# A gathered buffer holds rows of four heads for 32 tokens, TensorE sums all of V in four column tiles, VectorE makes every convolution

## The reference, cut to what matters

```
xbc = silu(causal_depthwise_conv(xbc, conv_w, conv_b))      # 4 taps, 4096 channels
...
h   = layer_norm(ALPHA * h + merged @ w_out)
...
hid = einsum('td,thkd->thk', xb, expert_u[ib])              # t tokens, 8 heads, 16 experts
act = gelu(hid) * gate
out = einsum('thk,thkd->td', act, expert_v[ib])
h   = layer_norm(ALPHA * h + out)
```

## Time and profile before

| what | value |
|---|---|
| median of 3 runs | 3692.26 us (3683.3 to 3696.73) |
| span of the profiled execution | 3689.4 us |
| PE busy | 3041.9 us, 82% |
| DVE busy | 2784.4 us, 75% |
| ACT, POOL busy | 1041.1 us, 2079.6 us |
| DMA moved | 1394.61 MB, 378 GB/s over the span |

### The profile page before, as it was taken

How to read it: one execution, slowest core, us unless ns; L and a number is a source line. 1 busy time by engine, 2 the same in 40 slices (tenths; PEclk the granted TensorE clock), 3 DMA queues, 4 the chain that set the end, 5 groups by cost and what they waited for, 6 DMA issues and landing times.

```text
span 3689.4 us, 41001 instructions
## 1 busy us (share of the span) xinstructions
PE 3041.9 (82%) x13528; PEld 2256.1 (61%) x13528; DVE 2784.4 (75%) x5841; ACT 1041.1 (28%) x2599; POOL 2079.6 (56%) x1839
## 2 busy tenths in 40 slices
PE   8984988988889899999988889999978974664665
PEld 7884877777778557877776537887765521221221
DVE  3318974988885898888777888888777886667666
ACT  5511542234331223444312114444211111111101
POOL 0004543566554667776666677677666676555553
PEclk9997998989999999999999999999999997887778
DMA  6658999999898999999999999999999999999997
GB/s 244 212 228 320 398 407 363 382 360 359 325 340 341 411 391 411 402 411 397 381 411 412 403 393 412 410 393 403 393 388 409 372 408 401 421 421 421 421 421 326
DMA packets 316546, 1394.61 MB, mean 378 GB/s; under 512 B 35376, under 2 KB 40880, under 8 KB 251824
## 3 DMA queue, kind: packets, MB, share of 16 engines
q0 software_dynamic: 262656, 1073.86, 73.4%
q1 hardware_dynamic: 52384, 313.42, 21.6%
q10 hardware_dynamic: 1296, 4.72, 0.3%
HBM read 1387.66 MB, written 4.19 MB: 377 GB/s over the span
## 4 chain that ended last, share of the span: by engine, by line
PE 30%; DMA 23%; POOL 9%; DVE 9%; issue 6%; ACT 2%; DVEq 1%; ACTq 0%; POOLq 0%
PE main L637 13%; DMA rowbuf<-ev,idx 9%; POOL rowbuf L594 6%; PE vbank L723 5%; DMA rowbuf<-euv,idx 4%; PE main L645 3%; DVE acc L1667 3%; DMA ring<-euv,idx 3%; PE main L848 2%; DVE rowbuf L1641 2%; PE main L833 2%; PE turn L708 2%; DMA xT<-euv,idx 2%; DMA merged<-euv,idx 2%; DMA rowbuf<-eu,idx 1%
## 5 line engine op out<-in xcount | busy, mean ns | idle before, releaser
L594 POOL DMA_INDIRECT rowbuf<-eu,idx x714 | 845.2, 1184 | 895.0 <-DVE hdot L1641 347.7
L594 POOL DMA_INDIRECT rowbuf<-ev,idx x713 | 773.7, 1085 | 323.1 <-issue 193.9
L1641 DVE CUSTOM_DVE_ANT_0 rowbuf<-rowbuf,hb 128x1024 f32<-128x1024 f32 x620 | 758.1, 1223 | 139.9 <-DMA rowbuf<-eu,idx 73.5
L637 PE MATMUL main<-xT,ring 128*128 128x256 f32 (+1 forms) x4480 | 802.8, 340 | 49.4 <-ACT mm L1104 38.9
L637 PEld LDWEIGHTS main<-xT,ring 128*128 128x128 f32 x4480 | 722.1, 193 | 124.1 <-issue 54.4
L723 PE MATMUL vbank<-rowbuf,vdiag 128*128 128x512 f32 x1152 | 602.4, 660 | 174.2 <-DMA rowbuf<-ev,idx 90.5
L1667 DVE SCALAR_TENSOR_TENSOR acc<-rowbuf,hact,acc 128x1024 f32<-128x1024 f32 x509 | 655.0, 1287 | 98.9 <-DMA rowbuf<-ev,idx 89.8
L723 PEld LDWEIGHTS vbank<-rowbuf,vdiag 128*128 128x128 f32 x1152 | 225.8, 210 | 490.6 <-issue 326.0
L1053 ACT ACTIVATE vdiag<-ident,hact 128x128 f32<-128x128 f32 x441 | 165.3, 396 | 515.2 <-DVE hact L1650 339.2
L833 PE MATMUL main<-late,ring 128*128 128x256 f32 (+1 forms) x1280 | 239.5, 352 | 36.0 <-issue 27.2
L833 PEld LDWEIGHTS main<-late,ring 128*128 128x128 f32 x1280 | 214.4, 203 | 60.4 <-issue 30.8
(11 more groups left out here) (249 smaller groups left out, 4136.3 us busy)
## 6 DMA issues: line engine op xcount, KB each, us to landing
ring<-wblocks SPq DMA_DIRECT2D x280, 1024.0 KB, 8.1
rowbuf<-eu,idx POOLq DMA_INDIRECT x714, 11.8
rowbuf<-ev,idx POOLq DMA_INDIRECT x713, 11.6
pw<-poolw SPq DMA_DIRECT2D x20, 256.0 KB
h_out<-acc ACTq DMA_DIRECT2D x8, 512.0 KB, 7.5
xT<-xt SPq DMA_DIRECT2D x3, 1024.0 KB, 16.8
zy<-x SPq DMA_DIRECT2D x3, 1024.0 KB, 13.9
craw_ln<-ln1g SPq DMA_DIRECT2D x5, 512.0 KB, 14.2
```

Of the source, the lines that this page charges most:

```text
L594: pool.indirect_dma_start(rows[r], None, (eu, ev)[table], bass.IndirectOffsetOnAxis(ap=idx[c % 2][:, u, k:k + 1], axis=0)).then_inc(row_re ...
L637: last = pe.matmul(dst_[:, ct * tc:(ct + 1) * tc], w[:, k, ct * P:(ct + 1) * P], src[:, k, 0:tc], start=(k == 0), stop=(k == KD - 1))
L1641: last = dve.tensor_tensor_reduce(r, r, h, 1.0, 0.0, ALU.mult, ALU.add, hdot[:, g % 2, k:k + 1])
```

## The change

**Layout.** A gathered buffer no longer holds one row for each of 128 tokens but rows of four heads for 32 tokens: partition 32a + m holds head a's row of token 32j + m. Four buffers j = 0 to 3 together (a quad, `QUAD`) cover the 128 tokens. The number of gathers, their bytes and their order in U and V stay.

**V.** VectorE makes from the weights of 16 slots one tile `spots` (128 x 512: for each slot 32 columns with the weight on the token's place). `sum_quad` on TensorE multiplies each of the four buffers by its 32 columns and adds into partitions 32j to 32j + 31 of `vbank`: eight matmuls of 128 x 512 moving data with 32 columns of weights each, for four buffers. At the start of a tile TensorE adds h itself into `vbank`. VectorE's `sum_row` and the diagonals of ScalarE are gone; `finish_tile` copies the banks.

**U.** `dot` now needs h in the new layout: `hp`, four parts j of 128 x 1024. TensorE makes each part with eight matmuls into `hbank` (`copy_rows`), ScalarE copies the two banks out (`copy_out`). Part j of the next tile is made when the dots that read the old one are done; `places_of_copies` puts it at the first place where the scan does not use `hbank`. The last tile has its own copy in `late`, so the paired rows have 14 buffers instead of 16.

**Experts and gates.** `choose` leaves expert numbers and gates by token in `choice`; TensorE moves them to the new layout (`move`, 16 small matmuls for each tile and half) and VectorE copies them out (`collect`). For the second half this comes in part A of the next chunk.

**Convolutions.** `convolve` and `conv_weights` are gone: chunks 3 and 4 do as chunks 0 to 2.

**Steps.** `WIDTHS` of chunk 3 goes from (124, 26, 16, 40, 38) to (128, 28, 16, 42, 42), so `END` goes from 780 to 792.

```diff
-WIDTHS = ((128, 28, 16, 42, 24), (40, 6, 6, 12, 12), (88, 16, 10, 34, 32), (124, 26, 16, 40, 38), (128, 28, 16, 42, 42))
+WIDTHS = ((128, 28, 16, 42, 24), (40, 6, 6, 12, 12), (88, 16, 10, 34, 32), (128, 28, 16, 42, 42), (128, 28, 16, 42, 42))
...
+            def copy_rows(t, j, scanned, moves):
+
+                if 0 < t < TILES - 1:
+                    pe.wait_ge(row_free, t * TILE - TOPK + QUAD * (j + 1))
+                pe.wait_ge(h_ready, t + 1)
+                pe.wait_ge(y_free, scanned + 1)
+                pe.wait_ge(st_used, scanned + STATE)
...
+                for half in range(2):
+                    n = 2 * (t * QUAD + j) + half
+                    if n >= 2:
+                        pe.wait_ge(hp_ready, n - 1)
+                    for a in range(QUAD):
+                        last = pe.matmul((ybank, stbank)[half][a * 32:(a + 1) * 32, :], ident[:, j * 32:(j + 1) * 32],
+                                         hb[:, t % NT, half * 512:(half + 1) * 512], start=True, stop=True)
+                    last.then_inc(hp_made, 1)
...
-            def convolve(c, j, n):
-
-                pe.wait_ge(conv_raw, (c - FILL) * 4 * AJ + j * 4 + n + 1)
...
-                first = q == PE_ORDER[0] or PE_ORDER[n - 1] // TILE < t
-                if first and t:
-                    pe.wait_ge(vsum_read, t)
-                pe.wait_ge(vdiag_ready, n + 1)
-                pe.wait_ge(ready, landed)
+            def sum_quad(q):
+
+                t, g = q // TILE, q // TOPK
...
+                pe.wait_ge(spots_ready, groups_before(q) + 1)
+                for j in range(QUAD):
+                    _, ready, landed = row(1, q + j)
+                    pe.wait_ge(ready, landed)
                 for half in range(2):
-                    last = pe.matmul(vbank[half][:, :], vdiag[:, n % DIAGS, :], r[:, half * 512:(half + 1) * 512],
-                                     start=first, stop=False, skip_group_check=True)
+                    for j in range(QUAD):
+                        r, _, _ = row(1, q + j)
+                        last = pe.matmul(vbank[half][j * 32:(j + 1) * 32, :], spots[:, g % 2, q % TOPK + j, :],
+                                         r[:, half * 512:(half + 1) * 512], start=False, stop=False, skip_group_check=True)
                 last.then_inc(row_free_pe, 1)
...
-                for t in range(nt):
-                    to = ds(t * PH + i * 4, 4)
-                    last = dve.tensor_copy(idx[c % 2][:, to, :], self_[:, t:n_u:nt, :])
...
+            def collect(c, i):
+
+                dve.wait_ge(moved, c * 2 + i + 1)
```

More of the change, by code:

```diff
@@ L140, in where, with order_rows @@
     return c, tile - FIRST[c], q // TOPK - FIRST[c] * PH
[L143 to L173 removed]
+def order_rows():
+    order, at = [], 0
@@ L174, in assign_rows @@
     for p in range(PAIRED + 1):
-        steps = [(0, p)] if p < PAIRED else []
+        if p < PAIRED:
+            order.append((0, p, False, p + 1))
         while at < PAIRED and step_of_v(at) == p:
-            steps.append((1, at))
+            order.append((1, at, True, at // QUAD + 1))
             at += 1
-        for table, q in steps:
-            by_pe = table == 1 and on_pe[q]
-            count[by_pe] += 1
-            order.append((table, q, by_pe, count[by_pe]))
-    pairs = []
@@ L220, in step_of, with freed @@
     return step_of_v(q) if table else q
+def freed(n):
+    table, q, _, _ = ORDER[n]
+    return step_of_quad(q) if table else q
 def guest_span(c, g):
@@ L596, in _ @@
                                         ).then_inc(row_ready[r], 16)
-            for n, (q, _, _) in enumerate(BOTH):
-                (c, _, u), k = where(q), q % TOPK
+            for n, q in enumerate(range(PAIRED, PAIRS)):
+                (c, _, u), k = where(q), column(0, q)
                 r = n % BOTHS
@@ L948, in _ @@
                 front_d(c)
+            move(NC - 1, 1, (NC, 0, 0))
+            for j in range(QUAD):
+                copy_rows(TILES - 1, j, scans(NC, 0, 0), NC * 2)
             until(PAIRS + LEAD2)
@@ L1067, in until @@
                 for o in range(at, p):
-                    for n, (_, first, begin, _) in enumerate(BANKED):
-                        if not first and o == begin - SETTLE + 1:
-                            bank_h(n)
                     g, k = divmod(o - 18, TOPK)
@@ L1282, in front_d @@
                 score(0, 3)
+                until(o(16))
+                if c == 0:
+                    for j in range(QUAD):
+                        copy_out(0, j)
                 until(o(35))
@@ L1318, in _ @@
                 front_d(c)
+            until(END)
+            for j in range(QUAD):
+                copy_out(TILES - 1, j)
             until(PAIRS + LEAD2 + 16)
```

468 lines of the change are left out of this document (208 added, 260 removed).

## The result

The changed kernel takes 3827.55 us (median of 4 runs, 3824.51 to 3837.86) against 3688.31 us (median of 4, 3683.3 to 3696.73) before: a ratio of 1.0384, 95% interval 1.0363 to 1.0405. The prediction of 3673 us was wrong, in sign too, and the time lies just above its range. The profiled execution has a span of 3827.1 us.

A forecast was written before the change was run, and what follows sets the result against it. It took the front to bound 694 to 1207 us and memory the paired rows, with engines and DMA close from 1406 to 3111. Terms summed to -19 us, giving 3673 us; 8-in-10 range 3640 to 3825.

The forecast's parts named there:

- start and later indices: Kernel start, `move` and `collect` ahead of the first gather: +4 us; first half of chunk 2's indices: +1.
- chunk 1: 390 to 630 us: 12 nearly all new quads, 24 us, on a TensorE idle for 37 of 240 us: +3.
- chunk 2, part A: New quads and copies of h against fewer waits and a quicker clock: 388 us for 390, -2.
- chunk 2, C and W: 6.5 quads, 13 us, replace 4 buffers' 8 us on a TensorE without idle time: +2.
- 1406 to 3111 us: Chunks 3 and 4, memory-bound: 682 MB at 406 instead of 400 GB/s, 1680 us for 1705, -25.
- paired rows: Paired rows, bound by memory at 421 GB/s: 14 buffers instead of 16 still leave several in flight, 0.
- tail: After the last dot: four sums of 5.3 us become `spots`, a quad and a copy, -2 us.
- What bounds the kernel: Whole kernel: front bounds 694 to 1207 us, engines and DMA close from 1406 to 3111, memory bounds paired rows at 421 GB/s.
- The quad: TensorE's sums of V: four buffers, 16 passes, taken as 2.0 us, between 1.7 side by side and 6.9 one by one.
- I take 406: Chunks 3 and 4, 1406 to 3111 us: engine relief lifts the rate from 400 to 406 GB/s, -25 us.
- rival (3): Single rows: V buffers held 8 to 10 us longer, fewer in flight, 392 GB/s, +35 instead of -25, 3733 us; chance 0.08.
- Its sign: From chunk 3 on: a rate below 397 GB/s with POOL waiting for TensorE would show held buffers.

The follow-up runs named there:

- `FILL` 5: Kernel before with VectorE also making the convolutions of chunks 3 and 4, nothing else changed: 3770.31 us, ratio 0.9979.
- The kernel with both costs: Kernel before, V buffers reused only after all four of a quad are read, dots always reading h from SBUF: 3896.75 us, ratio 1.0325; earlier run 3899.65.

## Why the prediction was wrong

Its terms beside what the two traces show (differences of the table's first two columns, taken before rounding; the other parts add 2 us ahead of chunk 1 and 4 us in chunk 2's D):

| term | forecast | measured |
|---|---|---|
| start and later indices | +5 | -1 |
| chunk 1 | +3 | +10 |
| chunk 2, part A | -2 | +20 |
| chunk 2, C and W | +2 | +19 |
| 1406 to 3111 us | -25 | +87 |
| paired rows | 0 | +1 |
| tail | -2 | -4 |

**What bounds the kernel**: right as far as it went, that from chunk 3 on it is memory, and that more TensorE time there is worth little. **The quad** of 2.0 us: right (1.92). So was TensorE's load in parts A (383 forecast, 395 and 388 measured) and that VectorE would fall to about 265 (272). `move` and `collect` are hidden: POOL's wait for the first indices is 279.6 us, as in the earlier trace rows. That 14 paired buffers do as well as 16: right.

**The step that failed** is "I take 406". It read the distance from 400 to 410 GB/s as something that the engines kept back. But the run with `FILL` 5 takes some 42 us of TensorE's busy time out of such a part and gains nothing, while taking two buffers away costs 1.2%, adding two gives 1.4, and holding V's by quads costs 3.4: the rate was set by how many gathers were under way. The term of -25 us measured +87. The prediction saw the opposing mechanism, as rival (3), with the right place and the right hold ("three steps or 8 to 10 us"; the mean from landing to reading of a quad's first buffer is 11.7 us, worked out over 1480 to 3200 us), and gave it 0.08. It argued that a gather "takes 11.6 us to land, mostly queueing, and can do with less". The gathers do land in 8.7 to 9.2 us now, but the rate fell with it, from 400 to 370 to 389 GB/s: that queue was not spare. In the twelve row buffers a V gather's whole round, from issue to the next issue into its buffer, went from 21.8 to 24.4 us, and a U gather's from 21.6 to 21.0. The rival's own price was too small as well: it said 392 GB/s and +35 us, the stretch shows 370 to 389 and +87, a part of which is not holding (below). Its sign, a rate below 397 with POOL waiting for TensorE, came true. The 157 us that POOL waited for TensorE were cited for it and then outweighed; with its waits for VectorE's dots, 386.9 us in the same view, which the prediction did not read, POOL had waited some 540 us for buffers already:

```profile
POOL rowbuf L594 <- DVE hdot L1641: 386.9, 182, 17.0
```

**Not seen at all**, a term put at nothing without a word, was the other part of those 87 us: that h in PSUM for the dots went with the change, and that GpSimd's issue has its own duration, 0.94 us at best, which with the 0.30 us between was never put against the 1.31 us that 512 KB take at 400 GB/s. On the quicker chip this costs the kernel before 1.3%, 52 us; it is clearest in chunk 4's D, where the change added 22 us and GpSimd is taken for 301 of 309.

**Chunk 2's part A**: the copies of h were costed at 18 us and set against two gains, 12 us of a quicker clock and the 36.9 us of waits ahead of L687 that would go. The clock did rise (0.92 to 0.96) and TensorE is 364 us busy of 395, fewer than the 378 forecast. But it now has 31 us of idle time for the 10 forecast, of it 18.5 in the scan and 7.5 for a landing:

```profile
PE hbank L695 <- issue: 18.5, 8, 4.3
PE vbank L727 <- DMA rowbuf<-ev,idx: 7.5, 1, 7.5
```

Without the copies this part takes 366 us, without copies and with two more buffers 362, its time before: the quads' 48 us and the relief cancelled, and the copies stood on top with 17, about the 18 that they were costed at. How much the part lost hangs on where it is cut: from the first projection of part A to the first matmul of part C it took 382 us and takes 393, +11, and steps 100 to 188 of the retrieval +20. Both lie within the 375 to 405 us that the prediction named, so the mechanism there was nearly right. **C and W of chunk 2**: +19 for +2. Ten of it come back with the gathers issued together or with two more buffers (145 to 135 us), and holding alone adds 10 to the old kernel (129 to 139): held buffers again; the rest was not traced. **Chunk 1**: its part A took 14 us more and what follows 4 less; holding alone adds 12 to that part A on the slower chips (171 to 183).

Held buffers were measured at more than the whole change where before takes 3783 us: 1.034 and 1.037 against 1.026, in a kernel that still picks its buffers in the old way. Whether the relief of both engines was worth anything is therefore not shown. The kernel with both costs takes 3897 us and the changed one 3883, on two chips of one level; with some 25 us for the copies of h (0.5 to 0.7%) about 40 us are left for the relief and the better choice of buffers together, by that estimate. That holding, put into the kernel before, is enough for the whole loss on the slower chips is shown, and so is the 1.3% of the slower issue on the quicker one; how the loss of 3.8% there divides between them is not.

None of the runs beats the kernel before; the nearest with the full computation are the old one with `FILL` 5, which is level, and the changed kernel with gathers together, 1.2% slower than before.

## What to carry to other kernels

When a change lets one instruction read several gathered buffers, price the hold: add up issue, landing, waiting and reading for one buffer and ask whether the number in flight still covers the queue; where the issuing engine stands idle for a reader at many reuses, it does not. Add up its waits for all readers, not for the one that the change touches. Take each issue's own duration times the number of issues as a load like any other, and ask whether another engine's operands, moved from PSUM to SBUF, make it longer. And where two engines look 95% busy beside a full DMA share, relieve one of them by a trivial edit first: if nothing happens, they were not the bound.

## What the runs showed of the hardware that was not expected

- Passes of 32-column matmuls in four column tiles run four at a time in either program order: 16 passes in 1.92 us at 2.4 GHz, against 6.9 us one by one, although every f32 matmul is two passes.
- An indirect gather's issue on GpSimd takes 0.94 us alone and 1.96 us in the row above beside a dot with both operands in SBUF; with h in PSUM the mean in the stretch above is 0.99 instead of 1.19 us.
- Chips differ by 2.6% on the same kernel (3688 and 3783 us), but by 0.9% on the kernel before without the copy in PSUM (3740 and 3775) and by 1.4% on the changed one (3828 and 3883). The paired rows take 560 to 562 us on each, so the difference lies ahead of them. Why was not found.
